# Delta rule's inverse in a hybrid decoder block: pairs of 64x64 products become block-diagonal 128x128 products

## The chip, the cores and the metric

The kernel runs on one core of a Trainium2 chip. The metric is the device time of one execution in microseconds (us); lower is better. The core has a matrix engine (PE, with its weight loads shown apart as PEld), a vector engine (DVE), a scalar engine (ACT), a general engine (POOL) and an engine that issues most of the DMAs (SP). Each runs its own instruction stream in order and waits for the others on semaphores.

## The reference, cut to what matters

One decoder block over 512 tokens of 1024 channels: a norm, an input projection, four heads of a gated delta rule beside four groups of causal pooling, an output projection with the residual, and a mixture of 32 experts (top 4). All arithmetic of the part below is float32. The change touches only the way in which `t_mat` is computed:

```python
n = t // CHUNK                      # 512 tokens in 8 chunks of 64
g = jnp.cumsum(heads_chunks(g), axis=-1)
strict = pos[:, None] > pos[None, :]
decay = jnp.exp(jnp.where(causal, g[..., :, None] - g[..., None, :], -jnp.inf))
k_beta = k * beta[..., None]
a_mat = jnp.where(strict, jnp.einsum('bhnid,bhnjd->bhnij', k_beta, k) * decay, 0.0)
t_mat = lax.linalg.triangular_solve(a_mat, eye, left_side=True, lower=True, unit_diagonal=True)
u = jnp.einsum('bhnij,bhnjd->bhnid', t_mat, v * beta[..., None])
w = jnp.einsum('bhnij,bhnjd->bhnid', t_mat, k_beta * jnp.exp(g)[..., None])
```

There are 4 heads and 8 chunks, so 32 triangles of 64x64. `t_mat` is the inverse of a lower triangle with ones on its diagonal.

## The kernel before, in words

**Layout.** A pair of heads shares the 128 partitions: head `2*hp + hh` lies on partitions `64*hh` to `64*hh + 63`. A tile such as `AT`, `TM`, `YM` or `TR` is 128 x 16 x 64: 16 columns `c = 2*n + hp` (chunk n, pair hp), each with two 64x64 blocks one above the other. `group(a)` is one half of them, 8 columns.

**The inverse.** `AT` holds the constant triangles, transposed. It starts from blocks of 2 (`TR`) and doubles the block in five levels (`LEVELS = 5`). A level s of a half a is five steps on three engines: PE multiplies `AT` with the turned inverse `TM` into a PSUM bank (`level_products`, L1538), DVE masks the result into `YM` (`level`, L1032), PE multiplies `YM` with the inverse `TR` into the next bank (`level_update`, L1543), ACT copies that negated into `TR` (`keep_inverse`, L684), and DVE turns it into `TM` (`turned`, L922). The last level's result goes through DVE's `columns_scaled` (L1037, L1038) instead. Both products go through `tiles` (L1529): for each of 8 columns one matmul for each hh, with 64x64 weights on the partitions of that head and 64 moving columns. A float32 matmul is two matmul instructions and two weight loads in the trace, so one half-level product shows as 32 instructions. Five levels, two halves and two products make 20 half-level products.

**The order.** PE's order is written out by hand. `project` (L1468) is the input projection, 8 matmuls of 128x128 weights by 512 columns for each of 20 column blocks; from block 10 to block 15 each is cut into two parts of 4 matmuls (8 instructions), and between the parts stand the half-level products, an update of one half behind a product of the other. So there are 11 stays in L1529: the first and the last hold one half-level product, the nine between hold two. Behind one of them stand 32 matmuls with one moving column (L1742, the norms of q), behind two others the transposition of v (L1522). Ahead of all stand the products of k and q (L1512), and behind them `u_rows`, `w_rows` and the sequential scan over the chunks. DVE's order is by hand too: between the levels it runs the short convolution of the projection's blocks (`conv`, L936).

**Behind the mixer** come the output projection (L1488), the router and the expert loop. The loop streams 384 pieces of 1 MB of expert weights through a ring of 20 slots (`ring`); slots are also the mixer's scratch memory, so the first pieces are loaded one by one as the mixer lets go of them, each load behind a wait of SP on a count of PE or DVE. Slot 0 isn't used by the mixer, and SP loads its piece (`load_unit(0, 0, 0)`) right after the small inputs.

**Names that the change touches.** `GUM`, `NG` and `BI` are POOL's spread tables of the decays, in the ring at 14336, 15360 and 16384; `prep_ps` counts PE's preparing products, `dx_ok` DVE's use of `NG`, `spread_ok` POOL's tables, `tr0_ok` the first inverse, `ym_ok` the masked products, `y_ps` and `tr_ps` PE's two products, `u_ps` the products of `u_rows`.

Of the kernel before, what the change touches and what calls it, by code (L numbers as in the profile page):

```python
# [18 lines left out]
P = 128  # L19
# [6 lines left out]
CH = 64  # L26
NCH = T // CH
NC = 2 * NCH
# [25 lines left out]
def moe_block(nc, x, attn_norm_w, w_in, conv_w, a_log, dt_bias, dn_norm_w, pool_w, pool_scale, w_out,  # L54
# [3 lines left out]
    with ctx:  # L58
# [10 lines left out]
        def room(at, *dims):  # L69
            n = 1  # L70
            for d in dims:
                n *= d
            flat = late[:, at:at + n]
            if len(dims) == 2:
                return flat.rearrange("p (a b) -> p a b", a=dims[0])
            if len(dims) == 3:
                return flat.rearrange("p (a b c) -> p a b c", a=dims[0], b=dims[1])
            return flat
# [8 lines left out]
        junk = room(14400, D)  # L87
        GUM, NG, BI, AT, TM, YM = [room(14336 + 1024 * i, NC, CH) for i in range(6)]
        KKD, TRv = YM, YM
        sqq = room(20480, H, T)  # L90
        VTOK = room(20480, NC, P)
        wout = room(14336, KD, D)
# [239 lines left out]
        def group(a):  # L332
            return slice(NC // 2 * a, NC // 2 * (a + 1))

        def colb(v, n):

            return bc(v, n, 2)

        def mask(v, n):

            return bc(v, n, 1)
# [3 lines left out]
        def _(sp):  # L345
# [20 lines left out]
            def load_unit(e, u, slot):  # L366
                sp.dma_start(unit_dst(slot, u), unit_src(e, u)).then_inc(slot_in[slot], 16)  # L367

            load_unit(0, 0, 0)
            sp.wait_ge(proj_ps, 2)  # L370
            load_piece(3)
            sp.wait_ge(bias_ok, 1)
# [9 lines left out]
                                 bc(zeros, TOPK, 1)).then_inc(zeroed, 16)  # L382
            sp.wait_ge(u_ps, 2)
            sp.dma_start(wout[:, :, :], w_out[0].rearrange("(k p) c -> p k c", p=P)).then_inc(wout_in, 16)
            sp.wait_ge(proj_ps, 18)
            load_unit(0, 8, 8)
            sp.wait_ge(pool_mix, 4)
# [85 lines left out]
        def _(pool):  # L473
# [55 lines left out]
            for n in range(3):  # L529
# [4 lines left out]
                else:  # L534
                    ins.then_inc(bias_ok, 1)

            pool.wait_ge(lvl_ok, 1)
            pool.wait_ge(g_ok, 1)
            G.tensor_tensor(GUM, mask(cz, NC), colb(gt[:, 8], CH), ALU.mult).then_inc(spread_ok, 1)
# [1 line left out]
            G.tensor_tensor(NG, mask(negC, NC), colb(gcs[:, 0], CH), ALU.subtract).then_inc(spread_ok, 1)  # L541
            pool.wait_ge(rr_ok, 1)
            G.tensor_tensor(BI, mask(identC, NC), colb(kcs[:, 0], CH), ALU.mult).then_inc(spread_ok, 1)

            pool.wait_ge(zeroed, TB * 16)
            for g, w in enumerate(WINDOWS):
# [322 lines left out]
        def _(dve):  # L869
# [50 lines left out]
            def turned(a):  # L920

                V.transpose(TM[:, group(a)].rearrange("p c f -> p (c f)"),  # L922
                            TR[:, group(a)].rearrange("p c f -> p (c f)")).then_inc(tm_ok, 1)
# [100 lines left out]
            for a in range(2):  # L1024
                dve.wait_ge(tr0_ok, a + 1)
                turned(a)
            conv(8)

            def level(s, a):

                dve.wait_ge(y_ps, 2 * s + a + 1)
                V.tensor_tensor(YM[:, group(a)], bank(2 + 2 * a, 8), mask(lvl[:, s + 1, :], 8), ALU.mult).then_inc(ym_ok, 1)  # L1032

            def columns_scaled(a):

# [390 lines left out]
        def _(pe):  # L1426
# [73 lines left out]
            def rows(hh):  # L1500
                return slice(CH * hh, CH * (hh + 1))
# [20 lines left out]
                            last = mm(pair_bank(6, P)[rows(hh), c], chunk_of(v, n, 2 * hp + hh), ident, start=True, stop=True)  # L1522
                last.then_inc(s, 1)

            def tiles(b, lhsT, rhs, a):

                for c in range(NC // 2):
                    for hh in range(2):
                        last = mm(bank(b, 8)[rows(hh), c], lhsT[rows(hh), NC // 2 * a + c, :], rhs(hh, NC // 2 * a + c),  # L1529
                                  start=True, stop=True)  # L1530
                return last

            def of(v):
                return lambda hh, c: v[rows(hh), c, :]

            def level_products(s, a):

                pe.wait_ge(tm_ok, 2 * s + a + 1)  # L1538
                tiles(2 + 2 * a, AT, of(TM), a).then_inc(y_ps, 1)

            def level_update(s, a):

                pe.wait_ge(ym_ok, 2 * s + a + 1)  # L1543
                tiles(3 + 2 * a, YM, of(TR), a).then_inc(tr_ps, 1)

            def u_rows(a):

# [475 lines left out]
```

## Time and profile before

| | us |
|---|---|
| median of 3 runs | 1320.4 |
| lowest and highest | 1319.56, 1321.78 |
| the profiled execution, device time | 1322.16 |
| its span, first to last instruction | 1318.7 |
| PE busy in the span | 1269.6 |
| DVE busy | 516.4 |
| ACT busy | 190.9 |
| POOL busy | 160.8 |

The profile is one execution. Its span is 3.5 us shorter than its device time, and that time is 1.8 us above the median. A page has the busy time of each engine, the span in 40 slices of 33 us, the chain of work that ended last, and groups of instructions by source line; a timeline has the instructions in order of time. The inverse stands in slices 4 and 5 (102 to 167 us), the expert loop from slice 10 on.

### The profile page before, as it was taken

The page shows a single profiled execution, that of the slowest core. Times are in us where ns is not written, and L with a number is a line of the kernel's source. Part 1 is how long each engine was busy: PE and PEld are TensorE (multiplying, and loading weights), DVE is VectorE, ACT ScalarE, POOL GpSimd, SP SyncE. Part 2 cuts the span into 40 slices and gives each one's busy share as a digit, 9 for nine tenths or more (in the row PEclk, how much of TensorE's full clock was granted, in tenths as well). Part 3 has the DMA queues.
Part 4 walks back from the last instruction along what each step waited for, and adds up shares of the span by engine and source line. Part 5 has one row for each costly group of instructions (what it writes and reads, how often), then busy time and mean ns, then how long its engine had stood idle before and what let it go on. Part 6 is the DMA issues. An engine that isn't in the chain of part 4 may idle for free.

```text
span 1318.7 us, 52719 instructions
## 1 busy us (share of the span) xinstructions
PE 1269.6 (96%) x21836; PEld 747.0 (57%) x21837; DVE 516.4 (39%) x1734; ACT 190.9 (14%) x439; POOL 160.8 (12%) x267
## 2 busy tenths in 40 slices
PE   8999999999999999999999999999999999998896
PEld 4545655445565655666566656656656655654453
DVE  6554223347343333333333333433433433422237
ACT  3431123332000000000000000000000000000002
POOL 4100430122101011011011011010110110100010
PEclk9999999999999999999999999999999999999989
DMA  7453131509999999999999999999999999999997
GB/s 234 141 186 126 33 129 50 221 33 360 402 415 409 416 405 417 410 416 415 417 409 417 417 417 410 418 411 418 412 412 414 416 416 411 416 417 419 417 421 302
DMA packets 96888, 455.73 MB, mean 346 GB/s; under 512 B 11057, under 2 KB 23018, under 8 KB 63498
## 3 DMA queue, kind: packets, MB, share of 16 engines
q1 hardware_dynamic: 92784, 445.69, 83.9%
q0 software_dynamic: 3888, 8.40, 1.7%
q8 instruction: 86, 1.41, 0.4%
q14 instruction: 24, 0.20, 0.0%
q10 hardware_dynamic: 106, 0.04, 0.0%
HBM read 432.53 MB, written 23.27 MB: 346 GB/s over the span
## 4 chain that ended last, share of the span: by engine, by line
DMA 52%; PE 43%; DVE 2%; issue 2%; SPq 1%; POOL 0%; DVEq 0%; ACT 0%; POOLq 0%; ACTq 0%
DMA ring<-in_w_gate_up_dram 32%; DMA ring<-in_w_down_dram 19%; PE ps L1892 12%; PE ps L1468 11%; PE ps L1944 5%; PE ps L1488 4%; PE ps L1858 2%; PE ps L1529 2%; PE ps L1522 1%; PE ps L1924 1%; PE ps L1430 0%; PE ps L1884 0%; SPq L367 0%; DVE ring L1421 0%; PE ps L1614 0%
## 5 line engine op out<-in xcount | busy, mean ns | idle before, releaser
L1892 PE MATMUL ps<-ring,cat 128*32 128x256 f32 x9856 | 554.8, 382 | 7.8 <-DMA ring<-in_w_gate_up_dram 7.8
L1892 PEld LDWEIGHTS ps<-ring,cat 128*32 128x32 f32 x9856 | 305.4, 111 | 226.6 <-DMA ring<-in_w_gate_up_dram 10.7
L1944 PE MATMUL ps<-ring,cat 128*32 128x256 f32 x4800 | 278.1, 381 | 15.9 <-DMA ring<-in_w_down_dram 15.8
L1944 PEld LDWEIGHTS ps<-ring,cat 128*32 128x32 f32 x4800 | 142.3, 110 | 122.6 <-DMA ring<-in_w_down_dram 20.9
L1468 PE MATMUL ps<-hbuf,ring 128*128 128x512 f32 x320 | 147.7, 608 | 1.7 <-DVE hbuf L917 1.7
L1262 DVE TENSOR_REDUCE wslot<-ps 128x2 f32<-128x6 f32 x75 | 12.3, 164 | 323.2 <-ACT cat L843 321.6
L596 POOL DMA_INDIRECT pair_rows_dram<-cat,rowi x73 | 72.7, 996 | 451.6 <-ACT cat L843 451.6
L835 ACT ACTIVATE cat<-cat 128x128 f32<-128x128 f32 x154 | 47.7, 310 | 528.9 <-DVE cat L1286 528.9
L1858 PE MATMUL ps<-hbuf,cat 128*32 128x256 bf16 x2432 | 104.7, 273 | 1.5 <-DVE cat L1386 1.5
L1468 PEld LDWEIGHTS ps<-hbuf,ring 128*128 128x128 f32 x320 | 58.9, 192 | 68.3 <-issue 66.6
L1286 DVE TENSOR_SCALAR cat<-ps 128x128 f32<-128x128 f32 x154 | 44.8, 291 | 134.5 <-PE ps L1892 134.3
L843 ACT ACTIVATE cat<-ps,wslot 128x256 f32<-128x256 f32 x75 | 35.5, 474 | 371.4 <-PE ps L1944 371.4
L1858 PE MATMUL ps<-aux,cat 128*32 128x256 bf16 x1216 | 86.8, 273 | 0.0
L1858 PEld LDWEIGHTS ps<-hbuf,cat 128*32 128x32 bf16 x2432 | 66.5, 97 | 17.5 <-DVE cat L1386 2.0
L592 POOL TENSOR_TENSOR rowi<-rowj,qcol 128x1 int32<-128x1 int32 x75 | 15.2, 202 | 416.4 <-DMA pair_rows_dram<-cat,rowi 387.6
L1381 DVE COPY selu<-E 96x32 bf16 x75 | 13.3, 177 | 124.5 <-issue 124.5
L1488 PE MATMUL ps<-ring,cat 128*128 128x512 f32 x128 | 58.5, 601 | 2.3 <-DVE ring L1177 1.4
L1386 DVE TENSOR_TENSOR cat<-iotaf,rank 128x512 bf16 x75 | 51.9, 692 | 12.0 <-DVE gie L1382 12.0
L1294 DVE STREAM_TRANSPOSE cat<-cat 128x128 f32<-128x128 f32 x154 | 48.0, 312 | 5.3
L1290 DVE SCALAR_TENSOR_TENSOR cat<-cat 128x128 f32<-128x128 f32 x154 | 45.0, 292 | 5.3
L1293 DVE TENSOR_TENSOR cat<-cat 128x128 f32<-128x128 f32 x154 | 45.0, 292 | 5.2
L1287 DVE TENSOR_SCALAR cat<-ps 128x128 f32<-128x128 f32 x154 | 43.2, 280 | 0.0
(363 smaller groups left out, 816.9 us busy)
## 6 DMA issues: line engine op xcount, KB each, us to landing
ring<-in_w_gate_up_dram SPq DMA_DIRECT2D x256, 1024.0 KB, 10.0
ring<-in_w_down_dram SPq DMA_DIRECT2D x128, 1024.0 KB, 10.2
ring<-in_w_in_dram SPq DMA_DIRECT2D x10, 1024.0 KB, 6.3
pair_rows_dram<-cat SPq DMA_DIRECT2D x4, 2048.0 KB, 10.9
ring<-pair_rows_dram SPq DMA_DIRECT2D x4, 2048.0 KB, 18.3
ring<-in_w_out_dram SPq DMA_DIRECT2D x1, 4096.0 KB, 12.7
ring<-in_x_dram SPq DMA_DIRECT2D x4, 512.0 KB, 5.3
x_rows_dram<-ring SPq DMA_DIRECT2D x2, 1024.0 KB, 10.5
```

The lines of the kernel that those rows point to most:

```text
L596: G.indirect_dma_start(out=into, out_offset=bass.IndirectOffsetOnAxis(ap=rowi[:, 0:1], axis=0), in_=ys, in_offset=None, bounds_check=limit ...
L835: A(sg[:, half], gc[:, half], ACT.Sigmoid, scale=ALPHA).then_inc(sg_ok, 1)
L1286: V.tensor_scalar(gc[:, half], ps[:, b, 0:P], LIMIT, None, ALU.min).then_inc(gc_ok, 1)
L1290: step(V.scalar_tensor_tensor(out=uc[:, half], in0=uc[:, half], scalar=1.0, in1=gc[:, half], op0=ALU.add, op1=ALU.mult), uc_step, n * 2 + 2)
L1293: step(V.tensor_tensor(act_[:, half], uc[:, half], sg[:, half], ALU.mult), act_ok, n + 1)
L1294: V.transpose(to[:, half], act_[:, half]).then_inc(told, by)
L1386: step(V.tensor_tensor(hot[:, :, :, :], slots, mine, ALU.is_equal), hot_ok, count)
L1468: last = mm(bank(m % 2), win[:, piece % 3, k, m % 2 * P:(m % 2 + 1) * P], hT[:, k, :], start=k == 0, stop=k == KD - 1)
L1488: last = mm(bank(n % 2), catT[:, k, b * P:(b + 1) * P], wout[:, k, 512 * half:512 * (half + 1)], start=i == 0, stop=i == KD - 1)
L1858: last = mm(ps[SLOTS * q:SLOTS * (q + 1), 2, 0:QD].rearrange("p (j i) -> p j i", i=SLOTS), hot[:, b, 0, :], rows, start=b == 0 and n == 0, ...
L1892: last = mm(ps[SLOTS * q:SLOTS * (q + 1), banks[half], 0:2 * P].rearrange("p (s j i) -> p s j i", s=2, j=4), x[:, SLOTS * u:SLOTS * (u + 1 ...
L1944: last = mm(ps[SLOTS * q:SLOTS * (q + 1), 1, 0:QD], actT[:, c // 4, SLOTS * (c % 4):SLOTS * (c % 4 + 1)], w[:, i, q * QD:(q + 1) * QD], st ...
```

## The change

Two new views of the ring are made. `ATd` (slot 0) and `YMd` (at 14336, over `GUM` and `NG`) are 128 x 16 x 128: in each column c the two 64x64 blocks lie on the diagonal of a 128x128 tile, and the rest is zero. POOL fills both with zeros, `ATd` ahead of `GUM` and `YMd` behind `BI`, once `NG` and `GUM` have been read. DVE copies `AT` into `ATd` once, in four instructions, and `level` writes the masked products into the diagonal blocks of `YMd` with two instructions of 64 partitions where it had one of 128. PE's `tiles` becomes `joined`: one matmul with 128x128 weights and 64 moving columns for each column c where there were two with 64x64 weights. Slot 0 is thereby in use until `u_rows`, so its piece is loaded behind `w_out`.

```diff
@@ -87,6 +87,8 @@
         junk = room(14400, D)
         GUM, NG, BI, AT, TM, YM = [room(14336 + 1024 * i, NC, CH) for i in range(6)]
         KKD, TRv = YM, YM
+        ATd = ring[:, 0:UNIT].rearrange("p (c f) -> p c f", c=NC)
+        YMd = room(14336, NC, P)
         sqq = room(20480, H, T)
         VTOK = room(20480, NC, P)
         wout = room(14336, KD, D)
@@ -366,7 +368,6 @@
             def load_unit(e, u, slot):
                 sp.dma_start(unit_dst(slot, u), unit_src(e, u)).then_inc(slot_in[slot], 16)
 
-            load_unit(0, 0, 0)
             sp.wait_ge(proj_ps, 2)
             load_piece(3)
             sp.wait_ge(bias_ok, 1)
@@ -382,6 +383,7 @@
                                  bc(zeros, TOPK, 1)).then_inc(zeroed, 16)
             sp.wait_ge(u_ps, 2)
             sp.dma_start(wout[:, :, :], w_out[0].rearrange("(k p) c -> p k c", p=P)).then_inc(wout_in, 16)
+            load_unit(0, 0, 0)
             sp.wait_ge(proj_ps, 18)
             load_unit(0, 8, 8)
             sp.wait_ge(pool_mix, 4)
@@ -534,6 +536,7 @@
                 else:
                     ins.then_inc(bias_ok, 1)
 
+            link(G.memset(ATd, 0.0))
             pool.wait_ge(lvl_ok, 1)
             pool.wait_ge(g_ok, 1)
             G.tensor_tensor(GUM, mask(cz, NC), colb(gt[:, 8], CH), ALU.mult).then_inc(spread_ok, 1)
@@ -541,6 +544,9 @@
             G.tensor_tensor(NG, mask(negC, NC), colb(gcs[:, 0], CH), ALU.subtract).then_inc(spread_ok, 1)
             pool.wait_ge(rr_ok, 1)
             G.tensor_tensor(BI, mask(identC, NC), colb(kcs[:, 0], CH), ALU.mult).then_inc(spread_ok, 1)
+            pool.wait_ge(dx_ok, 2)
+            pool.wait_ge(prep_ps, GROW)
+            G.memset(YMd, 0.0).then_inc(spread_ok, 1)
 
             pool.wait_ge(zeroed, TB * 16)
             for g, w in enumerate(WINDOWS):
@@ -1024,12 +1030,21 @@
             for a in range(2):
                 dve.wait_ge(tr0_ok, a + 1)
                 turned(a)
+            for a in range(2):
+                for hh in range(2):
+                    r = slice(CH * hh, CH * (hh + 1))
+                    V.tensor_copy(ATd[r, group(a), r], AT[r, group(a), :]).then_inc(tr0_ok, 1)
             conv(8)
 
             def level(s, a):
 
                 dve.wait_ge(y_ps, 2 * s + a + 1)
-                V.tensor_tensor(YM[:, group(a)], bank(2 + 2 * a, 8), mask(lvl[:, s + 1, :], 8), ALU.mult).then_inc(ym_ok, 1)
+                if s == 0:
+                    dve.wait_ge(spread_ok, BI_OK + 1)
+                for hh in range(2):
+                    r = slice(CH * hh, CH * (hh + 1))
+                    V.tensor_tensor(YMd[r, group(a), r], bank(2 + 2 * a, 8)[r], mask(lvl[:, s + 1, :], 8)[r],
+                                    ALU.mult).then_inc(ym_ok, 1)
 
             def columns_scaled(a):
 
@@ -1522,26 +1537,23 @@
                             last = mm(pair_bank(6, P)[rows(hh), c], chunk_of(v, n, 2 * hp + hh), ident, start=True, stop=True)
                 last.then_inc(s, 1)
 
-            def tiles(b, lhsT, rhs, a):
+            def joined(b, lhsT, rhs, a):
 
                 for c in range(NC // 2):
-                    for hh in range(2):
-                        last = mm(bank(b, 8)[rows(hh), c], lhsT[rows(hh), NC // 2 * a + c, :], rhs(hh, NC // 2 * a + c),
-                                  start=True, stop=True)
+                    last = mm(bank(b, 8)[:, c], lhsT[:, NC // 2 * a + c, :], rhs[:, NC // 2 * a + c, :], start=True, stop=True)
                 return last
 
-            def of(v):
-                return lambda hh, c: v[rows(hh), c, :]
-
             def level_products(s, a):
 
                 pe.wait_ge(tm_ok, 2 * s + a + 1)
-                tiles(2 + 2 * a, AT, of(TM), a).then_inc(y_ps, 1)
+                if s == 0:
+                    pe.wait_ge(tr0_ok, 2 * a + 4)
+                joined(2 + 2 * a, ATd, TM, a).then_inc(y_ps, 1)
 
             def level_update(s, a):
 
-                pe.wait_ge(ym_ok, 2 * s + a + 1)
-                tiles(3 + 2 * a, YM, of(TR), a).then_inc(tr_ps, 1)
+                pe.wait_ge(ym_ok, 2 * (2 * s + a + 1))
+                joined(3 + 2 * a, YMd, TR, a).then_inc(tr_ps, 1)
 
             def u_rows(a):
```

PE, the first three stays in the inverse, before:

```order
L1468 MATMUL ps<-hbuf,ring 128x512 x4
L1529 MATMUL ps<-ring 64x64 x16
L1468 MATMUL ps<-hbuf,ring 128x512 x4
L1529 MATMUL ps<-ring 64x64 x16
L1529 MATMUL ps<-cat,ring 64x64 x16
L1468 MATMUL ps<-hbuf,ring 128x512 x4
L1529 MATMUL ps<-ring 64x64 x16
L1529 MATMUL ps<-cat,ring 64x64 x16
```

And the same place with the change (L1483 is `project`, L1543 `joined`):

```order
L1483 MATMUL ps<-hbuf,ring 128x512 x4
L1543 MATMUL ps<-ring 128x64 x8
L1483 MATMUL ps<-hbuf,ring 128x512 x4
L1543 MATMUL ps<-ring 128x64 x8
L1543 MATMUL ps<-cat,ring 128x64 x8
L1483 MATMUL ps<-hbuf,ring 128x512 x4
L1543 MATMUL ps<-ring 128x64 x8
L1543 MATMUL ps<-cat,ring 128x64 x8
```

The order and the places are the same; each group has half as many matmuls, with all 128 rows of the array.

DVE, from the first turned inverse to the first level, before:

```order
L922 STREAM_TRANSPOSE ring<-cat 128x512 x2
L936 SCALAR_TENSOR_TENSOR ring<-ps,pcol,ring 128x511
...
L1047 TENSOR_TENSOR ring<-ring,pcol 128x256
L1051 TENSOR_TENSOR ring<-ps,cat 128x512 x2
L1032 TENSOR_TENSOR ring<-ps,aux 128x512 x2
L922 STREAM_TRANSPOSE ring<-cat 128x512
```

And with the change (L928 is `turned`, L942 `conv`, L1046 `level`):

```order
L928 STREAM_TRANSPOSE ring<-cat 128x512 x2
L1036 COPY ring<-ring 64x8x64 x4
L942 SCALAR_TENSOR_TENSOR ring<-ps,pcol,ring 128x511
...
L1062 TENSOR_TENSOR ring<-ring,pcol 128x256
L1066 TENSOR_TENSOR ring<-ps,cat 128x512 x2
L1046 TENSOR_TENSOR ring<-ps,aux 64x8x64 x4
L928 STREAM_TRANSPOSE ring<-cat 128x512
```

Four copies are new ahead of a convolution, and each half of a level is two instructions instead of one.

## Rows read from the trace of the kernel before

**Rows 1.** The page: busy shares, slices, and the chain that ended last by line.
```profile
PE 1269.6 (96%) x21836; PEld 747.0 (57%) x21837; DVE 516.4 (39%) x1734; ACT 190.9 (14%) x439; POOL 160.8 (12%) x267
...
DMA  7453131509999999999999999999999999999997
...
DMA 52%; PE 43%; DVE 2%; issue 2%; SPq 1%; POOL 0%; DVEq 0%; ACT 0%; POOLq 0%; ACTq 0%
```
**Rows 2.** Timeline of PE, 102 to 128 us: start, length, form, weights rows*columns, moving shape.
```profile
102.38 1.15 PE L1529 MATMUL ps<-ring 64*64 64x64 f32 x32
103.46 3.70 PE L1468 MATMUL ps<-hbuf,ring 128*128 128x512 f32 x8
107.09 1.15 PE L1529 MATMUL ps<-ring 64*64 64x64 f32 x32
...
109.10 3.70 PE L1468 MATMUL ps<-hbuf,ring 128*128 128x512 f32 x8
...
120.39 2.03 PE L1742 MATMUL ps<-ring 128*64 128x1 f32 x64
122.35 5.40 PE L1468 MATMUL ps<-hbuf,ring 128*128 128x512 f32 x8
127.68 1.15 PE L1529 MATMUL ps<-ring 64*64 64x64 f32 x32
```
**Rows 3.** Timelines of PEld and PE around L1699, 16 moving columns.
```profile
44.72 0.86 PEld L1699 LDWEIGHTS ps<-ring 128*128 128x128 f32 x7 [0.24 <-issue]
...
44.71 0.96 PE L1699 MATMUL ps<-ring 128*128 128x16 f32 x8
45.52 0.68 PE L1468 MATMUL ps<-hbuf,ring 128*128 128x512 f32 x1
```
**Rows 4.** Timeline of PE around L1638, 128 moving columns.
```profile
241.43 1.05 PE L1638 MATMUL ps<-ring 128*128 128x128 f32 x8
242.32 3.60 PE L1488 MATMUL ps<-ring,cat 128*128 128x512 f32 x8
245.75 1.05 PE L1638 MATMUL ps<-ring 128*128 128x128 f32 x8
```
**Rows 5.** The stretch of 122.3 to 126 us: busy of PE, PEld, DVE, ACT, POOL, granted clock, DMA share, GB/s.
```profile
122.30:126.00 3.70, 3.70 (x10) 1.65 (x8) 1.67 (x3) 0.63 (x1) 0.00 (x0) 0.54 0.23 81
```
**Rows 6.** Timeline of DVE, 90 to 111 and 161 to 164 us, with the idle time ahead.
```profile
90.70 2.31 DVE L936 SCALAR_TENSOR_TENSOR ring<-ps,pcol,ring 128x511 f32<-128x511 f32 x3 [1.26 <-ACT ring L654]
...
103.58 0.69 DVE L1032 TENSOR_TENSOR ring<-ps,aux 128x512 f32<-128x512 f32 x1 [2.04 <-PE ps L1529]
...
109.85 0.71 DVE L922 STREAM_TRANSPOSE ring<-cat 128x512 f32<-128x512 f32 x1 [0.87 <-ACT cat L684]
...
161.81 0.69 DVE L1037 TENSOR_TENSOR ring<-ps,aux 128x512 f32<-128x512 f32 x1 [4.30 <-PE ps L1529]
...
163.02 0.68 DVE L1032 TENSOR_TENSOR ring<-ps,aux 128x512 f32<-128x512 f32 x1
```
**Rows 7.** Timeline of POOL: a memset of 1024 elements, and the idle time ahead of two others.
```profile
11.57 0.95 POOL L526 MEMSET cat<- 128x1024 f32 x1
...
41.80 1.90 POOL L539 TENSOR_TENSOR ring<-aux,ring 128x1024 f32<-128x1024 f32 x1 [15.44 <-DVE ring L981]
...
134.17 1.04 POOL L551 TENSOR_TENSOR ring<-ring 128x512 f32<-128x512 f32 x1 [65.24 <-ACT ring L663]
```
**Rows 8.** Timeline of SP's DMA issues, 16 to 197 us.
```profile
16.25 2.28 SPq L367 DMA_DIRECT2D ring<-in_w_gate_up_dram  x1
...
179.50 0.37 SPq L384 DMA_DIRECT2D ring<-in_w_out_dram  x1
196.63 0.37 SPq L367 DMA_DIRECT2D ring<-in_w_down_dram  x1
```
**Rows 9.** Timeline of SP and PE where the output projection ends and the experts begin.
```profile
296.87 1.45 SPq L367 DMA_DIRECT2D ring<-in_w_down_dram  x3
...
307.34 2.78 PE L1892 MATMUL ps<-ring,cat 128*32 128x256 f32 x48
```

## The prediction, made before the changed kernel ran

> **What bounds the kernel now.** I read the page first. PE is busy for 1269.6 of 1318.7 us, and the chain that ended last is DMA for 52% and PE for 43%; the slices of the DMA engines show where each part lies: 9 from slice 9 or 10 on, where the expert weights stream, and mostly 5 or less before that [rows 1]. The change lies in the part before. So the second view is PE's timeline there. In the inverse PE has no idle time at all: each row starts before the one ahead of it has drained, and none carries a releaser [rows 2]. Each level's steps on ACT and DVE fit beside the half projections. In such a stretch the end moves by what PE's own instructions take, and a wait matters only if it is new. The third question is whether a shift there reaches the end. The weights that open the stream are issued at 296.87, behind the output projection, and the first expert product runs at 307.34 [rows 9]; both hang on PE's progress, and nothing ahead of them runs by the clock of a long transfer. I take the shift to reach the end in full.
>
> **The pace of the small products.** A length in the timeline has the drain in it, so I take differences of starts. The first stay in L1529 holds one half-level product, 32 instructions, and takes 103.46 - 102.38 = 1.08 us; the next holds two, 64 instructions, and takes 109.10 - 107.09 = 2.01 us [rows 2]. The rows have 64*64 weights: head 0 and head 1 of a column sit in different corners of the array and run as a pair, so a pair takes 2.01 / 32 = 0.063 us.
>
> With the change a column is one tile of 128*128 weights with 64 moving columns, and no pair is left. There is no such row before; two rows stand on both sides of it. With 16 moving columns (L1699) seven weight loads span 0.86 us, of which the last is 0.19: one each (0.86 - 0.19) / 6 = 0.112 us. The eight products take 45.52 - 44.71 = 0.81 us in all, since the first of them comes early [rows 3]. With 128 moving columns (L1638) eight take 242.32 - 241.43 = 0.89 us, 0.111 each [rows 4]. Between 16 and 128 columns the pace doesn't change, so it is the weight load that sets it, and 64 columns lie between. I take 0.112 us for each instruction but the first of a stay, for which I take 0.06 (it comes early, as in L1699, but has 64 columns to move).
>
> **PE's sum.** A stay with two half-level products has 32 instructions: 31 x 0.112 + 0.06 = 3.53 us for 2.01, so +1.52, and there are nine: +13.7. A stay with one has 16: 15 x 0.112 + 0.06 = 1.74 for 1.08, so +0.66, and there are two: +1.3.
>
> One thing comes back. Half a projection between two stays takes 107.09 - 103.46 = 3.63 us [rows 2]; the same eight instructions between two groups of full 128*128 tiles take 245.75 - 242.32 = 3.43 [rows 4]. So going from full tiles to corners and back costs 0.20 us, and with the change projections and inverse are all full tiles. Eleven half projections follow the stays: 11 x 0.20 = 2.2 saved. But L1742, twice L1522 and the `u_rows` behind the last one still use part of the array: four of the eleven keep half of the 0.20, and three times the step into such a group is now paid behind a stay, 0.1 each; the half projection ahead of the first stay saves 0.1. That is 2.2 - 0.4 - 0.3 + 0.1 = 1.6 saved. PE's sum: 13.7 + 1.3 - 1.6 = **+13.4 us**.
>
> The bounds: by the lower row a full tile costs 0.81 / 8 = 0.101, which gives 9 x (3.24 - 2.01) + 2 x (1.62 - 1.08) - 1.6 = +10.5; by the upper one, 0.112 throughout and nothing for the early first, 9 x 1.57 + 2 x 0.71 - 1.6 = +13.9. I stay near the upper end, because the lower row is low only by its one early product in eight, and here it is one in 32.
>
> The Trainium skill ("TensorE: Matmul & The Clock Gate", LDWEIGHTS) has a weight load cost its number of columns divided by 1.2, in ns, whatever the rows. That speaks against this change too: 53 ns for a corner of 64 columns, of which two load side by side, against 107 ns for the full tile. By its figure the sum would be about +11.8 us; the trace has 112, and I go by the trace.
>
> **The clock.** Behind L1742, whose 64 instructions move one column each, the granted clock falls: it is 0.54 on average from 122.3 to 126 us [rows 5], so half of 2.4 GHz, 1.2, for nearly all of it, and the half projection takes 127.68 - 122.35 = 5.33 us in place of 3.63 [rows 2]: 1.70 us. What stands ahead of L1742 gets sparser, so I expect this fall again, and it stands in both kernels. If it goes, the sum is +11.7; if the runs behind the median lack it and the change has it, +15.1.
>
> **DVE.** Four copies into `ATd` stand ahead of `conv(8)`. No row has this shape; between a 128x512 operation of 0.69 us [rows 6] and nothing, I take 0.69, 2.8 us for the four. DVE is idle for 1.26 us there [rows 6], so `conv(8)` ends up to 1.5 us later, near 94.5. The projection that waits for it starts at 98.75, just ahead of the first stay (102.38 less 3.63) [rows 2]. It is hidden with 4 us to spare. A level's mask becomes two instructions, each as long along the free axis as the one before: 1.3 to 1.4 us for 0.69. The update that needs it comes a half projection later: `level(0, 0)` starts at 103.58 and the update's stay at 107.09 [rows 2, 6]. The tightest place is the last: `columns_scaled(0)` starts at 161.81, `level(4, 1)` at 163.02 and lasts 0.68 [rows 6], so it ends 1.9 us behind the update; it will end some 2.6 behind, and the next update is due 3.43 behind. That leaves 0.8 us. The turned inverse ends at 110.56, 1.5 us behind the update's end at 109.10, and the next product is due 3.43 behind: 1.9 to spare [rows 2, 6]. Cost on the path: nothing. If a masking instruction of 64 partitions took 1.1 us or more, the last place alone would open, by some tenths.
>
> **POOL and SP.** A memset of 1024 elements takes 0.95 us [rows 7], so each new one, of 2048, some 1.9. The first falls into 15.4 us of idle time ahead of `GUM`, the second into 65 us behind `BI`, with the first level 30 us off [rows 7]. SP's load of slot 0 leaves 16.25, where the queue waits for PE next, and goes behind `w_out` at 179.50; SP's next issue is at 196.63, held by PE [rows 8]. Its 1 MB is wanted at 307.34 [rows 9]. Both cost nothing, and gain nothing, since PE waits for no weights there.
>
> **The total.** The profiled execution is 1322.2 us, a span of 1318.7 and 3.5 around it: with 13.4 it would be 1335.6. The median of the runs is 1.8 below it, so the forecast for a median is 1320.4 + 13.4 = **1333.8**.
>
> **The rivals.**
> *Each instruction keeps its price.* In the stays an instruction costs 2.01 / 64 = 0.031 us today; if that is a cost of issue, 320 instructions for 640 save 10.1 us, with the 1.6 of the switches 11.7: 1308.7. The mechanism turns from gain to loss at (9 x 2.01 + 2 x 1.08 + 1.6) / 320 = 0.068 us an instruction. For it speaks that L1742 costs the same 0.031 with one column (64 in 122.35 - 120.39) [rows 2]; against it both rows of full tiles, 0.101 and 0.111 [rows 3, 4]. The Trainium skill (same page, Back-to-back issue gap) has a floor of some 60 cycles, 25 ns, for any matmul of up to 64 columns, and would count this as a saving. Chance 3%.
> *A full tile keeps the pace of a pair*, 0.063: then only the switches count, 1318.8. Same rows against it. 3%.
> *The long stays bring the clock down.* They grow from 2.0 to 3.5 us with 64 columns moved in 112 ns. If each of the nine falls as behind L1742, up to 1.70 each more: up to 1349. Against it: L1742 moved one column an instruction, the stays move 64. 6%.
> *The shift is swallowed* before the stream, because the first expert weights hold the loop and not PE: 1320. Against it rows 9. 2%.
>
> **How the numbers follow.** The forecast has 86%. Its range runs from the low bound without the clock's fall (10.5 - 1.7 = 8.8) to the high one with it in the change alone (13.9 + 1.7 = 15.6), plus 1 for a new wait: 1329 to 1337. The other cases hold 14%, so the range need not reach them. A measurement of this kernel can tell about 0.2%, 2.6 us, from no change. Faster by more: 3% (the first rival). Within: 5%. Slower: 92%.
>
> **What would show it.** In the changed trace: a stay of 32 instructions from start to next start 3.5 us; half projections between stays 3.43; PE still without idle time from 102 to 180 us; `level` in two instructions of about 0.69; the expert stream issued at about 310 in place of 296.87. I am wrong if a full tile with 64 columns takes under 0.1 us, if the clock falls at several stays, or if a DVE row ends later than PE wants it.

## The result, and the profile after

| | before | changed |
|---|---|---|
| median, us (4 runs each) | 1319.98 | 1335.12 |
| lowest and highest | 1319.48 to 1321.78 | 1333.21 to 1338.19 |
| span of the profiled execution | 1318.7 | 1333.8 |
| its device time | 1322.16 | 1335.87 |

The ratio is 1.0109, with a 95% interval of 1.0093 to 1.0126: the change makes the kernel 1.1% slower. The medians of the table lie 15.1 us apart; the ratio, with its interval, is some 12 to 17 us. In a second job, on the kernel before of that job, the ratio was 1.0109 again (1.0090 to 1.0128). The forecast was 1333.8, with 1329 to 1337 as its range. One execution of the kernel before in the first job of the experiments took 3921.6 us and stands in no ratio.

The page of the changed kernel, its busy shares and the DMA slices, beside [rows 1]:

```profile
PE 1278.4 (96%) x21517; PEld 759.9 (57%) x21517; DVE 526.9 (40%) x1748; ACT 191.2 (14%) x439; POOL 166.1 (12%) x269
...
DMA  6453113416999999999999999999999999999997
```

PE has 319 recorded instructions fewer (320 were taken out) and is busy 8.8 us longer. Which engine is busy for what share says nothing of the cause; PE's timeline does. Its columns are start, length, engine, line, form, weights (rows*columns), moving shape; L1483 is the projection, L1543 the new product, L1565 the `u_rows` behind the inverse:

```profile
102.32 1.89 PE L1543 MATMUL ps<-ring 128*128 128x64 f32 x16
104.05 3.65 PE L1483 MATMUL ps<-hbuf,ring 128*128 128x512 f32 x8
107.54 1.89 PE L1543 MATMUL ps<-ring 128*128 128x64 f32 x16
109.27 1.95 PE L1543 MATMUL ps<-cat,ring 128*128 128x64 f32 x16
111.06 3.65 PE L1483 MATMUL ps<-hbuf,ring 128*128 128x512 f32 x8
...
125.16 2.03 PE L1754 MATMUL ps<-ring 128*64 128x1 f32 x64
127.12 5.40 PE L1483 MATMUL ps<-hbuf,ring 128*128 128x512 f32 x8
132.36 1.89 PE L1543 MATMUL ps<-ring 128*128 128x64 f32 x16
...
183.79 1.96 PE L1565 MATMUL ps<-ring 64*64 64x128 f32 x32
```

A stay with two half-level products lasts 111.06 - 107.54 = 3.52 us, where it lasted 2.01 [rows 2]; one with a single product 104.05 - 102.32 = 1.73, where it lasted 1.08. The half projection between two stays takes 107.54 - 104.05 = 3.49 for 3.63. PE has no idle time here either, and the weight loads fill the stay as well. This is the stay as a stretch: busy time of PE, PEld, DVE, ACT, POOL, granted clock, DMA share, GB/s:

```profile
107.54:111.06 3.52, 3.52 (x34) 3.52 (x32) 1.38 (x2) 0.69 (x1) 0.00 (x0) 1.00 0.03 12
```

From the first stay to `u_rows` it is 183.79 - 102.32 = 81.47 us. Before, `u_rows` started at

```profile
170.04 1.97 PE L1553 MATMUL ps<-ring 64*64 64x128 f32 x32
```

so 170.04 - 102.38 = 67.66 us: the inverse is 13.8 us longer, with one fall of the clock in either (5.24 us for a half projection here, 5.33 there).

The same shift stands where the experts begin. This is the first row of the expert products, which was at 307.34 [rows 9]:

```profile
320.94 2.78 PE L1904 MATMUL ps<-ring,cat 128*32 128x256 f32 x48
```

It is 13.6 us later; the weights that open the stream are issued at 310.63, which is 13.8 later than before. From that row to the end of the span it is 1333.8 - 320.94 = 1012.9 us, against 1318.7 - 307.34 = 1011.4 before. The stretch that doesn't belong to the change is thus 1.5 us longer in this pair of profiles; the section on the changed kernel's second run says whether that belongs to the change.

DVE's two new pieces, first the copies ahead of `conv(8)`, then the tightest place:

```profile
89.38 1.74 DVE L1036 COPY ring<-ring 64x512 f32<-64x512 f32 x4
91.15 2.32 DVE L942 SCALAR_TENSOR_TENSOR ring<-ps,pcol,ring 128x511 f32<-128x511 f32 x3
...
176.39 1.40 DVE L1046 TENSOR_TENSOR ring<-ps,aux 64x512 f32<-64x512 f32 x2
```

The convolution starts 0.45 us later than it did [rows 6], and the last mask ends at 177.79, 0.7 us ahead of the update at 178.48 that reads it. Neither holds PE.

### The profile page after: what moved, and what is told of

It is laid out like the page before. It is cut to its first block, busy times and chain, and to the rows that moved or that the text cites. A ratio compares the mean times of both kernels' runs of the same rounds, so it can differ in the third digit from the quotient of the medians.

```text
span 1333.8 us, 52101 instructions
## 1 busy us (share of the span) xinstructions
PE 1278.4 (96%) x21517; PEld 759.9 (57%) x21517; DVE 526.9 (40%) x1748; ACT 191.2 (14%) x439; POOL 166.1 (12%) x269
## 4 chain that ended last, share of the span: by engine, by line
PE 59%; DMA 37%; DVE 2%; issue 1%; SPq 0%; ACT 0%; DVEq 0%; POOL 0%; POOLq 0%; ACTq 0%
DMA ring<-in_w_gate_up_dram 22%; PE ps L1904 20%; DMA ring<-in_w_down_dram 13%; PE ps L1483 11%; PE ps L1956 10%; PE ps L1503 4%; PE ps L1870 4%; PE ps L1543 3%; DMA x_rows_dram<-cat,rowi 1%; PE ps L1896 1%; PE ps L1947 1%; PE ps L1537 1%; PE ps L1936 1%; PE ps L1879 1%; DMA ring<-in_x_dram 0%
## 5 line engine op out<-in xcount | busy, mean ns | idle before, releaser
L1904 PEld LDWEIGHTS ps<-ring,cat 128*32 128x32 f32 x9856 | 302.1, 110 | 226.6 <-DMA ring<-in_w_gate_up_dram 14.4
L1483 PE MATMUL ps<-hbuf,ring 128*128 128x512 f32 x320 | 147.3, 606 | 1.7 <-DVE hbuf L923 1.7
L1483 PEld LDWEIGHTS ps<-hbuf,ring 128*128 128x128 f32 x320 | 58.9, 192 | 67.8 <-issue 66.7
```

The source lines that it names most:

```text
L1483: last = mm(bank(m % 2), win[:, piece % 3, k, m % 2 * P:(m % 2 + 1) * P], hT[:, k, :], start=k == 0, stop=k == KD - 1)
L1904: last = mm(ps[SLOTS * q:SLOTS * (q + 1), banks[half], 0:2 * P].rearrange("p (s j i) -> p s j i", s=2, j=4), x[:, SLOTS * u:SLOTS * (u + 1 ...
```

## The experiments

The theory: a matmul with a full tile of 128x128 weights costs 0.112 us an instruction here because of its weight load, a pair of corners 0.063, and all else that the change brings is hidden. The rivals: DVE's doubled masks or the moved load carry part of it; the moving columns or the array's rows set the pace; the clock.

Ratios are to the kernel before as it ran in the same job, whose median was 1322.2 us in the first job, 1322.0 in the second and 1321.2 in the third. The expectations were written on a base of 1320, so I compare ratios.

### All of the change except PE's form

```diff
-                    last = mm(bank(b, 8)[:, c], lhsT[:, NC // 2 * a + c, :], rhs[:, NC // 2 * a + c, :], start=True, stop=True)
+                    for hh in range(2):
+                        last = mm(bank(b, 8)[rows(hh), c], lhsT[rows(hh), NC // 2 * a + c, rows(hh)],
+                                  rhs[rows(hh), NC // 2 * a + c, :], start=True, stop=True)
```

> The changed kernel, in which only PE's form is taken back: each column is again two matmuls with 64x64 weights, read out of the diagonal blocks of ATd and YMd. Both memsets, the four copies, the split masks and the late load of slot 0 stay. Theory (a full tile of 128x128 weights costs 0.112 us an instruction, a pair of corners 0.063, and all else is hidden): the time falls back to that of the kernel before, 1320.0 (within 0.7), and a stay with 64 instructions takes 2.01 us again. Rival (part of the 15 us is DVE's doubled masks, POOL's memsets or the late load): it stays above 1322.

Measured: 1321.0 us, a ratio of 0.9995 (0.9984 to 1.0006). The stay on PE's timeline is back at 109.34 - 107.33 = 2.01 us:

```profile
107.33 1.15 PE L1544 MATMUL ps<-ring 64*64 64x64 f32 x32
108.31 1.10 PE L1544 MATMUL ps<-cat,ring 64*64 64x64 f32 x32
109.34 1.13 PE L1483 MATMUL ps<-hbuf,ring 128*128 128x512 f32 x2
```

Memsets, copies, split masks and the late load together cost nothing that can be measured (the interval leaves room for 0.8 us). The loss is in PE's form.

### One half of the change: products full, updates in corners

```diff
-                joined(3 + 2 * a, YMd, TR, a).then_inc(tr_ps, 1)
+                for c in range(NC // 2):
+                    for hh in range(2):
+                        at = NC // 2 * a + c
+                        last = mm(bank(3 + 2 * a, 8)[rows(hh), c], YMd[rows(hh), at, rows(hh)], TR[rows(hh), at, :],
+                                  start=True, stop=True)
+                last.then_inc(tr_ps, 1)
```

> Half of the change: level_products with the full tiles of ATd, level_update with 64x64 corners read out of YMd; all else as in the changed kernel. Theory (0.112 us an instruction for a full tile, 0.031 for a corner, 0.1 to enter the corners and 0.1 to leave them): a stay with both products takes 1.73 + 0.09 + 1.01 = 2.83 us where it was 2.01 and 3.52, which over nine stays, the first one (1.73) and the half projections behind (3.54 for 3.63) makes +7.1 us over the kernel before, 1327.1 (1326 to 1328.5). Rival (the price is the switch between tile sizes and not the full tile's pace): more than the changed kernel, 1335 or above, because each stay now has a switch inside it too.

Measured: 1329.4 us, a ratio of 1.0066 (1.0043 to 1.0088), 5.7 to 11.6 us over the kernel before; the forecast of 7.1 lies in it, and the time is below that of the full change, whose interval it doesn't touch. The timeline gives the parts:

```profile
107.24 1.89 PE L1543 MATMUL ps<-ring 128*128 128x64 f32 x16
109.06 1.15 PE L1559 MATMUL ps<-cat,ring 64*64 64x64 f32 x32
110.14 3.70 PE L1483 MATMUL ps<-hbuf,ring 128*128 128x512 f32 x8
113.68 1.89 PE L1543 MATMUL ps<-ring 128*128 128x64 f32 x16
```

Full product and step into the corners 1.82 us, corners 1.08, half projection 3.54. Full tiles followed by full tiles took 1.73, so entering the corners costs 0.09; the 1.08 and 3.54 hold what leaving them costs. The switch is real and small; it is not what the change pays for. The stay takes 110.14 - 107.24 = 2.90 us for an expected 2.83, and the inverse of this profile 175.76 - 102.02 = 73.74 us without a fall of the clock, against 65.96 in the run with the late load below: 7.8 us for an expected 7.1. This profile also has a fall of the clock behind the inverse, which costs it 1.4 us (see the last experiment).

### All 128 rows, cut into two column halves

```diff
-                    last = mm(bank(b, 8)[:, c], lhsT[:, NC // 2 * a + c, :], rhs[:, NC // 2 * a + c, :], start=True, stop=True)
+                    for hh in range(2):
+                        last = mm(bank(b, 8)[rows(hh), c], lhsT[:, NC // 2 * a + c, rows(hh)],
+                                  rhs[:, NC // 2 * a + c, :], start=True, stop=True)
```

> The changed kernel with all 128 rows of the block-diagonal tile, but cut into two matmuls of 64 weight columns each (128x64 weights, one for each head's half of the outputs). Theory (the load goes by weight columns, and two column halves load side by side): a pair takes 0.063 us as the corners do, a stay of 64 instructions 2.0 us, total 1320 (1319 to 1321). Rival (the load or the product goes by rows times columns, or by the array being used in all its rows): a pair costs as much as the full tile, 0.112 or more, and the time is 1335 or above.

Measured: 1320.6 us, a ratio of 0.9993 (0.9983 to 1.0002).

```profile
107.17 1.15 PE L1544 MATMUL ps<-ring 128*64 128x64 f32 x32
108.16 1.10 PE L1544 MATMUL ps<-cat,ring 128*64 128x64 f32 x32
109.19 3.70 PE L1483 MATMUL ps<-hbuf,ring 128*128 128x512 f32 x8
```

The stay is 2.02 us. This kernel multiplies the same block-diagonal tiles by the same operands as the changed one, zeros included, and is as fast as the kernel before. Neither the zeros nor the rows cost anything; what costs is to load all 128 columns as one weight tile instead of two halves side by side.

### Twice the moving columns

```diff
-                    last = mm(bank(b, 8)[:, c], lhsT[:, NC // 2 * a + c, :], rhs[:, NC // 2 * a + c, :], start=True, stop=True)
+                    at, n = NC // 2 * a + c, 2 if c < NC // 2 - 1 else 1
+                    last = mm(bank(b, 8)[:, c:c + n].rearrange("p c f -> p (c f)"), lhsT[:, at, :],
+                              rhs[:, at:at + n, :].rearrange("p c f -> p (c f)"), start=True, stop=True)
```

> The changed kernel with the same weights, but 128 moving columns in seven of eight matmuls where it has 64: each also multiplies the next column's block, and the next matmul writes over that. Theory (the pace is set by the weight load, 0.112 us, and 128 columns fit into it): the same time as the changed kernel, 1335 (within 1.5), a stay of 32 instructions 3.5 us. Rival (the pace is set by the moving columns or the work in the array): seven eighths of the 320 instructions take up to twice as long, +20 to +30 us, 1355 or more.

Measured: 1333.8 us, a ratio of 1.0094 (1.0078 to 1.0110), as the changed kernel within both intervals.

```profile
107.25 1.89 PE L1544 MATMUL ps<-ring 128*128 128x128 f32 x16
108.98 1.95 PE L1544 MATMUL ps<-cat,ring 128*128 128x128 f32 x16
110.76 3.65 PE L1483 MATMUL ps<-hbuf,ring 128*128 128x512 f32 x8
...
318.95 2.78 PE L1906 MATMUL ps<-ring,cat 128*32 128x256 f32 x48
```

The stay is 3.51 us with twice the moving columns. So the changed kernel could move twice the columns in the same time. This run excludes the moving columns as what sets the pace, the one with two column halves the rows, and the first rival's count of instructions fell with the changed kernel; what is left is the number of weight columns that one instruction loads. The Trainium skill ("TensorE: Matmul & The Clock Gate", LDWEIGHTS) gives columns divided by 1.2, so 107 ns for 128 and 53 for 64, whatever the rows; the trace agrees in kind with 0.112 and, for a pair of halves, 0.063 per two instructions. Its floor of 25 ns for any small matmul (same page, Back-to-back issue gap), the ground of the forecast's first rival, doesn't show in these stays: 320 instructions fewer brought no gain. The same section says itself that its gaps are those of single matmuls and come out too low at few columns, since they leave out the load; the trace agrees with that, 112 ns for 25.

### The late load alone

The kernel before with `load_unit(0, 0, 0)` moved behind `w_out`, as in the change.

> The kernel before with one edit of the change alone: the load of slot 0 goes behind w_out. Theory (nobody waits for that megabyte, nor for the queue that it leaves): 1320.0 on the base of 1320.0, a ratio between 0.999 and 1.001. Rival (an early load is worth something later, or it held up the first projections): a difference of 1 us or more either way.

Measured: 1321.0 us, a ratio of 0.9995 (0.9985 to 1.0006). Its timeline has the first stay and `u_rows` at

```profile
102.73 1.15 PE L1529 MATMUL ps<-ring 64*64 64x64 f32 x32
...
168.69 1.96 PE L1553 MATMUL ps<-ring 64*64 64x128 f32 x32
```

which makes 65.96 us for the inverse, without a fall of the clock; the kernel before took 67.66 with one. The difference is the 1.70 us of that fall. The load is free at either place, within the 2 us that the interval leaves.

### The changed kernel again

> The changed kernel itself, in more rounds. Of its first profile the experts began 13.6 us later than before, and its span was 15.1 us longer. Theory (the change costs what it costs in the inverse, 13.7 us, and what is above that is the spread of the expert stream and of the clock from one execution to the next): the difference to the kernel before is 13.7 us, a ratio of 1.0104 (1.0095 to 1.0112). Rival (the shift also makes the expert stream longer, by 1.5 us or more): a ratio of 1.0115 or above.

Measured: 1336.3 us, a ratio of 1.0109 (1.0090 to 1.0128). The interval holds both 1.0104 and 1.0115, so the ratio doesn't decide. The inverse of this second profile has no fall of the clock and takes 183.67 - 103.89 = 79.78 us, against 65.96 in the run with the late load, which has none either: 13.8 us, as in the pair with a fall in each. Its span is not shorter for it, because it began the inverse 1.6 us later (103.89 for 102.32); its granted clock was 0.91 on average in the first 20 us, where it was 1.00 in the first profile.

Whether the stream behind grows with the shift, all eleven profiles tell: from the first row of the expert products to the end of the span it is

| kernel | first expert row | span | between |
|---|---|---|---|
| before | 307.34 | 1318.7 | 1011.4 |
| late load alone | 306.00 | 1317.8 | 1011.8 |
| half | 314.47 | 1326.3 | 1011.8 |
| changed, norms in two groups (below) | 322.85 | 1335.3 | 1012.4 |
| changed, again | 320.82 | 1333.6 | 1012.8 |
| changed | 320.94 | 1333.8 | 1012.9 |
| twice the columns | 318.95 | 1332.0 | 1013.1 |
| all but PE's form | 307.44 | 1320.6 | 1013.2 |
| two column halves | 305.17 | 1318.4 | 1013.2 |
| four corners (below) | 303.38 | 1316.8 | 1013.4 |
| norms in two groups (below) | 305.67 | 1319.6 | 1013.9 |

Six profiles are of kernels as fast as the one before or faster, four of kernels with full tiles in both products; the stretch is 1012.8 on average in either group, so it doesn't grow with the shift. The profile of before has the shortest of all, and the 1.5 us are spread. The shift reaches the end one to one.

### The clock

> The kernel before, with the 32 matmuls of one moving column each (the norms of q) in two groups of 16, the second one half projection later, behind the next stay in the inverse. Theory (the long row of one-column matmuls brings the granted clock down for 3.4 us behind it, which costs 1.7 us in the profiled execution): the clock stays at 2.4 GHz there, a switch between full tiles and half tiles is not added, and the time falls by 1.7 where the fall came, so 1318.3 to 1319.5. Rival (the fall hits whatever stands there, by something else than those matmuls): the clock still falls and the time stays 1320.0.

```diff
+            norms(0, NCH // 2)
             project(12, 0, 4)
             level_products(2, 0)
             level_update(1, 1)
+            norms(NCH // 2, NCH).then_inc(prep_ps, 1)
```

(`norms(lo, hi)` is the loop over n of the one-column matmuls.) Measured: 1319.8 us, a ratio of 0.9991 (0.9980 to 1.0001); no fall in the inverse of its profile. That separates nothing, because the undivided group brought none either in six other profiles. In the run with twice the columns the stretch behind it had the full clock (columns: stretch, busy of PE, PEld, DVE, ACT, POOL, granted clock, DMA share, GB/s):

```profile
124.90:126.80 1.90, 1.90 (x65) 1.90 (x64) 1.16 (x2) 0.60 (x1) 0.00 (x0) 1.00 0.68 237
126.90:130.30 3.40, 3.40 (x9) 1.56 (x9) 1.69 (x3) 0.63 (x1) 0.00 (x0) 1.00 0.00 0
```

The same edit on the changed kernel:

> The changed kernel with the 32 matmuls of one moving column in two groups of 16, the second behind the next stay. Theory (the long row of them, behind a stay of full tiles with few moving columns, is what brings the clock down in the changed kernel's inverse): no fall of the clock between 100 and 185 us, and where the fall came 1.7 us less; 0.1 us more for one more switch; so 1332 to 1334 against 1333.7. Rival (the stays themselves bring it down): the clock still falls somewhere in the inverse.

Measured: 1335.9 us, a ratio of 1.0099 (1.0082 to 1.0116), so no gain, and in its profile two falls where one was expected to vanish:

```profile
125.19 1.15 PE L1756 MATMUL ps<-ring 128*64 128x1 f32 x32
126.27 5.29 PE L1483 MATMUL ps<-hbuf,ring 128*128 128x512 f32 x8
131.40 1.90 PE L1543 MATMUL ps<-ring 128*128 128x64 f32 x16
133.13 1.95 PE L1543 MATMUL ps<-cat,ring 128*128 128x64 f32 x16
135.01 1.10 PE L1756 MATMUL ps<-ring 128*64 128x1 f32 x32
136.04 5.40 PE L1483 MATMUL ps<-hbuf,ring 128*128 128x512 f32 x8
```

```profile
126.20:129.50 3.30, 3.30 (x8) 1.56 (x7) 2.69 (x4) 0.47 (x1) 0.00 (x0) 0.50 0.06 17
129.60:136.20 6.60, 6.60 (x70) 5.47 (x69) 1.83 (x3) 0.65 (x2) 0.00 (x0) 1.00 0.00 0
136.40:139.70 3.30, 3.30 (x5) 1.35 (x4) 0.42 (x3) 0.00 (x0) 0.00 (x0) 0.50 0.02 5
```

The theory that the length of the one-column group matters has fallen: behind a stay of full tiles, a group of half the length brings the clock to 1.2 GHz too, and dividing it made two such places. The half projections take 131.40 - 126.27 = 5.13 and 141.28 - 136.04 = 5.24 us for 3.54, so the falls cost 1.6 and 1.7 us, as before. In all eleven profiles no fall came in the inverse except behind a one-column group: one in the kernel before, one in the changed kernel, one in the kernel with corners on the new tiles, two here. The changed kernel's second profile had none in the inverse. What decides from one execution to the next is left open: whether the group brings the fall or only stands where one can come, these runs don't separate. The long stays by themselves didn't bring one down in the four profiles that have them.

### All four corners of the array

If loads go by their columns and lie side by side, the kernel before uses only two of four corners. In `level_update` of the first four levels the odd columns can send their result to the other half of the partitions; a level later those columns work on that side, and come back. `level_products` then needs `AT` for them with its halves exchanged, a copy by two small DMAs.

```diff
+                        sp.dma_start(ATs[CH * (1 - i):CH * (2 - i)],
+                                     AT.rearrange("p (c o) f -> p o c f", o=2)[CH * i:CH * (i + 1), 1]).then_inc(ats_in, 16)
...
-                A(TR[:, group(a)], bank(3 + 2 * a, 8), ACT.Copy, scale=-1.0).then_inc(tr_ok, 1)
+                A(TR[:, group(a)].rearrange("p (c o) f -> p o c f", o=2),
+                  ps[:, 2 + 2 * a:4 + 2 * a, 0:256].rearrange("p o (c f) -> p o c f", f=CH),
+                  ACT.Copy, scale=-1.0).then_inc(tr_ok, 1)
...
+                        left = ATs[rows(x), at // 2, :] if c % 2 and s % 2 else AT[rows(x), at, :]
...
+                        if s == LEVELS - 1:
+                            out = bank(3 + 2 * a, 8)[rows(x), c]
+                        elif c % 2:
+                            out = bank(3 + 2 * a, 8)[rows(1 - x), c // 2]
+                        else:
+                            out = bank(2 + 2 * a, 8)[rows(x), c // 2]
+                        last = mm(out, YM[rows(x), at, :], TR[rows(x), at, :], start=True, stop=True)
```

> The kernel before with its 64x64 corners, and in level_update of the first four levels all four corners of the array in use: the odd columns send their result to the other half of the partitions (head 0's to 64 to 127 and back a level later), into a PSUM bank of their own, and level_products takes AT for them from a copy with its halves exchanged, made by two small DMAs. The number of instructions is that of the kernel before. Theory (a load's time goes by its 64 columns, and loads into different corners run side by side, as in the run with two column halves of 128 rows, where each instruction loads twice the rows at the same 0.031 us): four corners take 0.063 us as two do, an update of a half level 0.5 us instead of 1.0, eight of them save 4.0 us: 1316 on a base of 1320, a ratio of 0.997. Rival (two rows of corners don't run side by side when both column halves are in use, or the instruction stream itself costs 0.031 us an instruction): no gain, a ratio of 1.000, an update still 1.0 us.

Measured: 1318.7 us, a ratio of 0.9982 (0.9971 to 0.9993). PE's timeline, with the update in L1559:

```profile
102.41 1.15 PE L1544 MATMUL ps<-ring 64*64 64x64 f32 x32
...
107.12 1.09 PE L1544 MATMUL ps<-ring 64*64 64x64 f32 x30
108.00 0.27 PE L1559 MATMUL ps<-cat,ring 64*64 64x64 f32 x2
108.04 0.22 PE L1544 MATMUL ps<-ring 64*64 64x64 f32 x2
108.10 0.63 PE L1559 MATMUL ps<-cat,ring 64*64 64x64 f32 x30
108.67 3.70 PE L1477 MATMUL ps<-hbuf,ring 128*128 128x512 f32 x8
...
164.64 1.96 PE L1569 MATMUL ps<-ring 64*64 64x128 f32 x32
```

A stay is 108.67 - 107.12 = 1.55 us for 2.01, with the same 64 instructions. The update of before took 32 x 0.031 = 1.0 us (1.03 by the starts, 109.10 - 108.07); it now takes 0.46 less, some 0.54 to 0.57 for 32 instructions, so 0.067 to 0.071 for each four. The inverse takes 164.64 - 102.41 = 62.23 us against the 65.96 of the run with the late load, both without a fall of the clock: 3.7 us less, eight times 0.46 to 0.47. So it is not the number of instructions either that sets 0.031 us, and this version beats both kernels.

The whole program gained less than the 4.0 us expected: by the ratio 2.4 us (0.9 to 3.8). Its profile shows where the rest went, in part: from `u_rows` to the first expert row it is 303.38 - 164.64 = 138.74 us, against 306.00 - 168.69 = 137.31 in the run with the late load. In the router, ahead of the experts, the granted clock fell to half here and stayed full there:

```profile
292.00:294.00 2.00, 0.85 (x19) 0.43 (x17) 1.62 (x4) 0.63 (x4) 0.00 (x0) 0.93 0.94 291
294.00:296.00 2.00, 2.00 (x3) 0.78 (x4) 0.75 (x2) 1.75 (x3) 0.00 (x0) 0.50 0.84 305
```

The profile with half of the change has the same fall and 138.71 us; the nine others have 137.15 to 137.31. PE was busy for 0.85 of the 2 us ahead of it; the same pauses stand in the run with the late load, without a fall. How many of the other executions had this fall is not known, so its part in the median isn't either. The Trainium skill ("TensorEngine Tiling (Array Packing)", Key Properties) says that different tiles load and multiply in parallel; the trace agrees, for two tiles and for four.

## Why the prediction was right

**PE as the bound, and the shift to the end.** Right. PE had no idle time in the inverse before or after, and the experts began 13.6 us later; the stretch behind didn't change beyond its spread (table above).

**The pace of a full tile.** Right, and the step that carried the result. The rows with 16 and with 128 moving columns [rows 3, 4] gave 0.112 and 0.111; the change gave (3.52 - 0.06) / 31 = 0.112, and without the assumed 0.06, from a double and a single stay, (3.52 - 1.73) / 16 = 0.112. That the rows on both sides agreed was the evidence that the weight load sets the pace; it left open a fixed cost of any instruction with a full tile. The runs with twice the moving columns and with two column halves showed that the pace goes by the weight columns of an instruction.

**PE's sum.** Forecast +13.4. Counted over the same stretch, from the half projection ahead of the first stay (98.75 before, 98.78 now) to `u_rows`, it is (183.79 - 98.78) - (170.04 - 98.75) = +13.7. A stay was forecast at 3.53 and measured 3.52, a single one 1.74 and 1.73. What the switches give back was oversized, 1.6 us for 1.1: I took 3.43 for a half projection between full tiles, from a group with 128 moving columns [rows 4], and it was 3.49, seven times and once more in the part ahead of `u_rows` (3.58 for 3.53). That is 0.5 us by which the sum should have been higher; stays that were some 0.01 shorter than forecast took back 0.1, and rounding did the rest. The weight loads show what goes with the 0.06:

```profile
102.32 1.75 PEld L1543 LDWEIGHTS ps<-ring 128*128 128x128 f32 x15 [0.24 <-issue]
103.99 0.30 PEld L1483 LDWEIGHTS ps<-hbuf,ring 128*128 128x128 f32 x2
```

and, in the kernel before,

```profile
242.21 0.30 PEld L1488 LDWEIGHTS ps<-ring,cat 128*128 128x128 f32 x2
```

Behind a stay the projection's first load begins 0.06 us ahead of its first matmul (103.99 and 104.05), behind L1638 it began 0.11 ahead (242.21 and 242.32), so more of that load is still to be done when the row starts. That this is the cause of the 0.06 is argued and not tested.

**The clock.** I expected the fall of the kernel before in the changed one again. It came in one profile of the changed kernel and not in the other; the bounds had allowed for either. That it is not there in every execution I had not seen, and none of the runs shows why. The forecast of the time didn't hang on it, since the pair of profiles had one fall each.

**DVE, POOL, SP.** Right that none costs anything (0.9995 with all of them kept). The four copies took 1.7 us together for my 2.8, the split mask 1.40 for 1.3 to 1.4, and the tightest place kept 0.7 us for my 0.8 (`level(4, 1)` ended at 163.70, 2.0 us behind the update's end at 161.70 and not 1.9).

**The rivals.** That an instruction keeps its price fell with the changed kernel, and the four corners show why: 64 instructions can take 1.55 us or 2.01. That a full tile keeps the pace of a pair fell with the timeline, 0.112 for 0.063. The long stays brought no fall of the clock. The shift was not swallowed.

**The total.** 1333.8 forecast, 1335.1 measured; as a difference 13.4 forecast and 14.4 by the ratio, with some 2 us either way. Of the 1 us between, the profiles account for 0.3, the switch less what the stays took back, and the rest is within what the runs can tell.

## What to carry to other kernels

Before joining two small products into one block-diagonal tile, look in the trace for how far apart the starts of full tiles stand at few moving columns: where that is the same at 16 and at 128 columns, as here with 0.112 and 0.111 us, the weight load is the first suspect for what sets the pace. Half as many matmuls with twice the weight columns then gained nothing and lost the overlap of the halves, 13.8 us in this inverse. A count of instructions is not a price. Small products that use two corners of the array are worth spreading over all four before they are joined; here that took 3.7 us out of the inverse.

## What the runs showed of the hardware that I had not expected

Four 64x64 float32 instructions in the four corners took hardly longer than two: 0.067 to 0.071 us for four, where a pair took 0.063, though two of the four send their result to the other half of the partitions than the one they read. The clock's fall behind the one-column group is not a fixed part of a kernel: the same group had it in some executions and not in others, and two groups of half the length had it twice in one. The same holds for the router, where the granted clock fell to 0.50 in two of eleven profiles and cost 1.4 us there; a difference of 1 or 2 us between two profiles of this program is first to be looked for in such falls.
